# Gated-DeltaNet heads: z's sigmoid behind q's, k finished ahead of v's convolution, filler cells in other places

## The chip, the cores and the metric

The kernel runs on one core of a Trainium2 chip. The metric is the device time of one execution in microseconds (us); a kernel's time is the median of several runs. Engines are named as in the profile: TensorE (PE, and PEld for its weight loads), VectorE (DVE), ScalarE (ACT), GpSimd (POOL) and SyncE (SP).

## What is computed

Two layers of a backbone over 640 tokens (128 of context, 512 latent) of width 2048. In each layer one input projection feeds three groups of heads: four gated-DeltaNet heads (GDN), eight latent-attention heads and four mLSTM heads; an output projection joins them. The change is in the GDN heads, but for one wait. A GDN head takes q, k, v and z (128 features by 640 tokens each) out of the projection:

```python
qkv = jax.nn.silu(_centred_dwconv(jnp.concatenate([qa, ka, va], axis=-1), p['gdn_conv']).astype(f32))
q, k, v = jnp.split(qkv, [H_A * DK_A, 2 * H_A * DK_A], axis=-1)
q = _l2norm(_heads(q, H_A))
k = _l2norm(_heads(k, H_A))
...
a = jnp.where(strict, jnp.einsum('bhncd,bhnsd->bhncs', kb, k) * decay, 0.0)
t = lax.linalg.triangular_solve(a + eye, jnp.broadcast_to(eye, a.shape),
                                left_side=True, lower=True, unit_diagonal=True)
...
out = _unheads(o) * jax.nn.silu(za.astype(f32))
```

The convolution has five taps along the tokens. The inverse of a + 1, forward and backward in time, is what a head waits for before its recurrence.

## The kernel before

Every engine's program is written out by hand, in order, and engines meet at semaphores. `B.wait(engine, label)` holds the engine's queue until the other engine has done the step with that label; `B.did` marks a step, and `B.link` marks it and lets the own queue wait for its end.

**The filler.** TensorE is kept busy with the projection of the head to come: four tiles (q, k, v, z) of sixteen *cells* each. A cell is six products of 320 columns (L587 to L589); in some cells a side product (L553, four small ones) follows, eight in a tile of layer 0 and four in one of layer 1. `ahead.cells(n)` (L571) puts the next n of the 64 cells at that place of TensorE's queue, `ahead.finish()` (L810) the rest. The tiles take two banks in turn, so tile 2 (cell 32) needs `take` 0 on ScalarE (L1206), which copies tile 0 out of its bank. GpSimd splits each half of a tile's weights in two parts before TensorE can use it (L489, L494).

**A head, in order.** ScalarE issues four DMAs (L1192, L1194: the states, and two rows broadcast to all partitions), then copies q, k and v into padded tiles (L1197, L1198) once VectorE has zeroed their edges (L1620 to L1622). VectorE convolves (L1631, L1633; five steps each), ScalarE makes a sigmoid of three steps (L1080 to L1082, called at L1201, L1208, L1218), VectorE multiplies the two (`silu`, L1640, L1641). ScalarE squares q and k (L1203, L1210), TensorE sums the squares over the features (`column_sums`, L625, L626: `q sum` into wa, `k sum` into wb), ScalarE makes `q rstd` and `k rstd` (L1100, L1101), VectorE multiplies (L1650, L1652). TensorE turns k and v (L620, into wa and wb), ScalarE copies them out (L1220, L1222; the second is `v turned taken`), and VectorE begins its chain into the inverse: decays of both directions (L1661 to L1666), then the products kk and qk (TensorE, L604 in `each_tile`) times the decays (L1674, L1676), then the first block matrices of both directions, `level00` and `level10` (L1682). The solve follows: ten rounds of small block products (L613 in `each_block`), and two levels of whole products (L604), with VectorE between (L1686 to L1713). The recurrence and `o sum` (L814) end a head. In the old order TensorE's cells stand thus: 16, `q sum`, 4, `k sum`, 4, k turned, 1, v turned, 5, kk and qk, 7, the block rounds with 10, then 2, and 1 at `finish`; the ones that the change does not touch make up the 64.

**The gates**, ahead of the heads in each layer: TensorE projects four tiles (L705 to L708), the second into a bank that held the gates' own projection, which ScalarE reads in four steps (L1153 to L1156) and works on up to `log` (L1160).

## Time and profile before

| | |
|---|---|
| median of 3 runs | 3312.5 us (3311.53 to 3313.3) |
| the profiled execution | 3306.19 us, its span 3304.4 us |
| TensorE busy | 3095.8 us, 94% |
| GpSimd busy | 2080.8 us, 63% |
| VectorE busy | 1246.6 us, 38% |
| ScalarE busy | 827.9 us, 25% |
| granted TensorE clock, mean | 0.983 |

The span runs from the first to the last instruction of one profiled execution. TensorE's busy time is nearly the span, so the rest of the reading is about its idle time: which group of instructions it stood before, and what ended the wait.

### The profile page before, as it was taken

How to read it: one execution, taken by the hardware profiler on the slowest of the kernel's cores; microseconds unless marked ns; L12 is line 12 of the kernel's file. 1: busy time of each engine (PE TensorE's matmuls, PEld its weight loads, DVE VectorE, ACT ScalarE, POOL GpSimd, SP SyncE). 2: the span in 40 equal slices, each digit the busy share in tenths (PEclk: the TensorE clock that was granted, in tenths of full speed). 3: DMA queues.
4: the chain of work that ended last, by engine and by line, in shares of the span. 5: the costliest groups of instructions: out<-in, count | busy, mean ns of one | idle time of the engine just before them, and what ended most of it. 6: DMA issues, size and time to landing. Idle time of an engine off the chain costs nothing. (4 is left out here: it accounts for less than half of the span.)

```text
span 3304.4 us, 64727 instructions
## 1 busy us (share of the span) xinstructions
PE 3095.8 (94%) x27490; PEld 2791.8 (84%) x27490; DVE 1246.6 (38%) x2462; ACT 827.9 (25%) x1698; POOL 2080.8 (63%) x2507
## 2 busy tenths in 40 slices
PE   6899999999999999999997999999999999999996
PEld 1488888789999997879986988888999999787996
DVE  1245556533222114442126456655333311345112
ACT  1413423411111222331015323333111122233000
POOL 3284533546666886537877734644788788653886
PEclk9999999999999999999998999999999999999998
DMA  8533433424444221103222322322232222111322
GB/s 325 193 98 106 144 105 104 140 75 117 128 135 131 74 72 58 45 33 112 77 100 72 118 77 80 100 76 69 77 84 83 84 74 72 58 39 33 118 77 112
DMA packets 122034, 319.93 MB, mean 97 GB/s; under 512 B 18256, under 2 KB 27600, under 8 KB 120592
## 3 DMA queue, kind: packets, MB, share of 16 engines
q1 hardware_dynamic: 91008, 263.38, 25.3%
q10 hardware_dynamic: 30736, 52.40, 4.6%
q8 instruction: 216, 3.54, 0.4%
q14 instruction: 74, 0.61, 0.1%
HBM read 302.65 MB, written 13.08 MB: 96 GB/s over the span
## 5 line engine op out<-in xcount | busy, mean ns | idle before, releaser
L489 POOL TENSOR_SCALAR w_hi<-raw 128x256 fp32r<-128x256 f32 x1232 | 1066.5, 891 | 1163.8 <-PE projection L589 684.2
L494 POOL TENSOR_TENSOR w_lo<-raw,w_hi 128x256 fp32r<-128x256 f32 x1232 | 964.3, 813 | 0.0
L587 PE MATMUL projection<-h_hi,w_hi 128*128 128x320 f32 x2304 | 762.9, 331 | 7.0 <-ACTq L1323 4.0
L589 PE MATMUL projection<-h_hi,w_lo 128*128 128x320 f32 x2304 | 714.7, 310 | 0.2 <-issue 0.2
L588 PE MATMUL projection<-h_lo,w_hi 128*128 128x320 f32 x2304 | 713.9, 310 | 0.0
L534 PE MATMUL projection<-h_hi,w_hi 128*128 128x320 f32 x1984 | 616.3, 311 | 21.2 <-POOLq L499 19.0
L535 PE MATMUL projection<-h_lo,w_hi 128*128 128x320 f32 x1984 | 613.8, 309 | 0.0
L536 PE MATMUL projection<-h_hi,w_lo 128*128 128x320 f32 x1984 | 613.6, 309 | 0.0
L587 PEld LDWEIGHTS projection<-h_hi,w_hi 128*128 128x128 f32 x2304 | 435.8, 189 | 50.6 <-issue 44.1
L588 PEld LDWEIGHTS projection<-h_lo,w_hi 128*128 128x128 f32 x2304 | 436.6, 189 | 0.3 <-issue 0.3
L589 PEld LDWEIGHTS projection<-h_hi,w_lo 128*128 128x128 f32 x2304 | 434.8, 189 | 0.0
L534 PEld LDWEIGHTS projection<-h_hi,w_hi 128*128 128x128 f32 x1984 | 374.0, 188 | 24.9 <-issue 16.6
L535 PEld LDWEIGHTS projection<-h_lo,w_hi 128*128 128x128 f32 x1984 | 374.1, 189 | 0.0
L536 PEld LDWEIGHTS projection<-h_hi,w_lo 128*128 128x128 f32 x1984 | 374.0, 188 | 0.0
L1934 DVE TENSOR_SCALAR xo<-projection,mul 128x128 f32<-128x128 f32 (+2 forms) x96 | 36.3, 434 | 373.4 <-ACT work L1450 373.4
L1096 ACT ACTIVATE xo<-projection 128x640 f32<-128x640 f32 x80 | 56.6, 707 | 303.7 <-PE projection L589 196.0
L1450 ACT ACTIVATE work<-projection 128x640 f32<-128x640 f32 x32 | 22.6, 707 | 419.6 <-PE projection L536 419.6
L553 PE MATMUL projection<-fill,cond 128*32 128x128 f32 x2048 | 109.7, 286 | 2.0 <-DMA fill<-in_w_fill 2.0
L897 PE MATMUL wb<-h_hi,w_hi 128*128 128x320 f32 (+1 forms) x296 | 100.2, 338 | 9.2 <-POOLq L499 9.2
L1898 DVE TENSOR_REDUCE row_sums<-projection 128x1 f32<-128x640 f32 (+1 forms) x80 | 57.4, 718 | 133.2 <-PE projection L955 131.8
L1417 ACT ACTIVATE work<-projection,row_sums 128x640 f32<-128x640 f32 (+1 forms) x80 | 56.9, 711 | 174.6 <-DVE row_sums L1899 174.6
L978 PE MATMUL wa<-work 128*128 128x128 f32 x672 | 90.3, 278 | 9.6 <-ACT work L1424 9.6
(399 smaller groups left out, 4338.4 us busy)
## 6 DMA issues: line engine op xcount, KB each, us to landing
raw<-in_w_stream SPq DMA_DIRECT2D x308, 512.0 KB, 3.4
fill<-in_w_fill SPq DMA_DIRECT2D x256, 256.0 KB, 2.7
work<-in_w_ada SPq DMA_DIRECT2D x64, 512.0 KB, 5.1
work<-rows ACTq DMA_DIRECT2D x32, 320.0 KB, 4.1
xo<-rows ACTq DMA_DIRECT2D x32, 320.0 KB, 5.1
xo<-in_x ACTq DMA_DIRECT2D x1, 5120.0 KB, 16.7
work<-in_x ACTq DMA_DIRECT2D x16, 320.0 KB, 5.1
x_kept<-xo ACTq DMA_DIRECT2D x4, 1280.0 KB, 4.5
```

The lines of the kernel that those rows point to most:

```text
L489: nc.gpsimd.tensor_scalar(w_hi[:, s, cs, :], raw[:, s, cs, :], 1.0, None, ALU.mult).then_inc(split_part, 1)
L494: nc.gpsimd.tensor_tensor(w_lo[:, s, cs, :], raw[:, s, cs, :], w_hi[:, s, cs, :].bitcast(F32), ALU.subtract).then_inc(split_part, 1)
L534: mm(o, w_hi[:, half, c, :], h_hi[:, tile, hs], start=(k == 0), stop=False)
L535: mm(o, w_hi[:, half, c, :], h_lo[:, tile, hs], start=False, stop=False)
L536: last = mm(o, w_lo[:, half, c, :], h_hi[:, tile, hs], start=False, stop=(k == KT - 1))
L553: last = mm(bank[g * COND_W:(g + 1) * COND_W, a, HALF:HALF + P], cond[:, quad * ROW_GROUPS + g, :], fill[:, s, g, :], start=False, stop=(q ...
L587: mm(o, w_hi[:, half, c, :], h_hi[:, k, hs], start=(k == 0), stop=False)
L588: mm(o, w_hi[:, half, c, :], h_lo[:, k, hs], start=False, stop=False)
L589: last = mm(o, w_lo[:, half, c, :], h_hi[:, k, hs], start=False, stop=(k == KT - 1))
L897: mm(out, hi, xh, start=first, stop=False)
L978: last = mm(wa[:, 768:768 + P], values4[:, k0 + j, vs], T(probs_t[i % 2], j), start=(j == 0), stop=(j == nk - 1))
L1898: B.link(V.reduce_max(mxs[:, 0, t:t + 1], MLA_SCORES[i % 2][:, 0:nk], AX))
```

## The change

In the gates the second tile's projection waits for `beta exp` (L1156) where it waited for `log`. In a GDN head the four DMA issues stand behind the padding copies; z's sigmoid stands behind q's; k's square follows q's, `k rstd` comes ahead of v's sigmoid and `q rstd` behind it; `take` 0 goes behind `q rstd`. VectorE makes k's `silu` ahead of v's convolution, and norms k before v's `silu`. TensorE turns k into wb and v into wa, and v's turn waits for `q rstd` too, which reads wa. The cells stand as 16, `q sum`, 1, `k sum`, 4, k turned, 2, v turned, 2, kk and qk, 9, the block rounds with 10, then 4, and 2 at `finish`.

```diff
                     if j:
-                        B.wait("act", "log" if j == 1 else f"ahead taken{j - 2}")
+                        B.wait("act", "beta exp" if j == 1 else f"ahead taken{j - 2}")
...
                     B.did(column_sums(wa, wt(9)), "q sum")
-                    ahead.cells(4)
+                    ahead.cells(1)
                     B.wait("act", "k squared")
                     B.did(column_sums(wb, wt(11)), "k sum")
                     ahead.cells(4)
                     B.wait("dve", "k normed")
-                    B.did(transposed(wa, wt(1)), "k turned")
-                    ahead.cells(1)
+                    B.did(transposed(wb, wt(1)), "k turned")
+                    ahead.cells(2)
                     B.wait("dve", "v silu")
-                    B.did(transposed(wb, wt(4)), "v turned")
-                    ahead.cells(5)
+                    B.wait("act", "q rstd")
+                    B.did(transposed(wa, wt(4)), "v turned")
+                    ahead.cells(2)
                     B.wait("act", "v turned taken")
                     B.did(each_tile(wa, wt(1), wt(1)), "kk")
+                    B.wait("dve", "q normed")
                     B.did(each_tile(wb, wt(1), wt(0)), "qk")
-                    ahead.cells(5)
-                    ahead.cells(2)
+                    ahead.cells(9)
...
                         ahead.cells(1)
-                    ahead.cells(2)
+                    ahead.cells(4)
...
-                    for d in range(2):
-                        act.dma_start(gdn_state(d), io["state_gdn"][l, d, h, :, :]).then_inc(state_in[d], 16)
-                    for tile, kind in ((row_g[0], 0), (row_beta[0], 1)):
-                        act.dma_start(tile, rows[kind, bass.ds(h, 1), :].partition_broadcast(P)).then_inc(rows_in[0], 16)
                     B.wait("dve", "zeros")
                     for i in range(3):
                         B.did(A(pads[i][:, 2:2 + CTX], xt(4 + i)[:, 0:CTX], ACT.Copy))
                         B.did(A(pads[i][:, 6 + CTX:6 + TOK], xt(4 + i)[:, CTX:TOK], ACT.Copy), f"{'qkv'[i]} padded")
+                    for d in range(2):
+                        act.dma_start(gdn_state(d), io["state_gdn"][l, d, h, :, :]).then_inc(state_in[d], 16)
+                    for tile, kind in ((row_g[0], 0), (row_beta[0], 1)):
+                        act.dma_start(tile, rows[kind, bass.ds(h, 1), :].partition_broadcast(P)).then_inc(rows_in[0], 16)
                     for i in range(2):
                         B.wait("dve", f"{'qk'[i]} conv")
                         sigmoid(B, pads[i][:, 0:CONVW], convs[i], f"{'qk'[i]} sigmoid")
+                        if i == 0:
+                            sigmoid(B, xt(9), xt(7), "z sigmoid")
                     B.wait("dve", "q silu")
                     B.did(A(wt(9), wt(0), ACT.Square), "q squared")
-
+                    B.wait("dve", "k silu")
+                    B.did(A(wt(11), wt(1), ACT.Square), "k squared")
+                    for tile, kind in ((row_g[1], 0), (row_beta[1], 1)):
+                        act.dma_start(tile, rows[kind, bass.ds(h + 4, 1), :].partition_broadcast(P)).then_inc(rows_in[1], 16)
+                    B.wait("pe", "k sum")
+                    rsqrt(B, wt(12), wb[:, 0:TOK], wt(12), 1.0, "k rstd")
+                    B.wait("dve", "v conv")
+                    sigmoid(B, pads[2][:, 0:CONVW], convs[2], "v sigmoid")
+                    B.wait("pe", "q sum")
+                    rsqrt(B, wt(10), wa[:, 0:TOK], wt(10), 1.0, "q rstd", DK_SCALE)
                     B.wait("act", "v padded")
                     take(B, n0_, 0, xt(4))
-                    B.wait("dve", "v conv")
-                    sigmoid(B, pads[2][:, 0:CONVW], convs[2], "v sigmoid")
-                    B.wait("dve", "k silu")
-                    B.did(A(wt(11), wt(1), ACT.Square), "k squared")
-                    B.wait("pe", "q sum")
-                    rsqrt(B, wt(10), wa[:, 0:TOK], wt(10), 1.0, "q rstd", DK_SCALE)
-                    B.wait("pe", "k sum")
-                    rsqrt(B, wt(12), wb[:, 0:TOK], wt(12), 1.0, "k rstd")
-
-                    for tile, kind in ((row_g[1], 0), (row_beta[1], 1)):
-                        act.dma_start(tile, rows[kind, bass.ds(h + 4, 1), :].partition_broadcast(P)).then_inc(rows_in[1], 16)
-                    sigmoid(B, xt(9), xt(7), "z sigmoid")
                     B.wait("pe", "k turned")
-                    B.did(A(wt(2), wa[:, 0:TOK], ACT.Copy))
+                    B.did(A(wt(2), wb[:, 0:TOK], ACT.Copy))
                     B.wait("pe", "v turned")
-                    B.did(A(wt(3), wb[:, 0:TOK], ACT.Copy), "v turned taken")
+                    B.did(A(wt(3), wa[:, 0:TOK], ACT.Copy), "v turned taken")
...
                     silu(0, wt(0))
+                    silu(1, wt(1))
                     conv(2)
-                    silu(1, wt(1))
+                    B.wait("act", "k rstd")
+                    B.did(tt(wt(1), wt(1), wt(12), ALU.mult), "k normed")
                     silu(2, wt(4))
                     B.wait("act", "q rstd")
                     B.did(tt(wt(0), wt(0), wt(10), ALU.mult), "q normed")
-                    B.wait("act", "k rstd")
-                    B.link(tt(wt(1), wt(1), wt(12), ALU.mult), "k normed")
```

ScalarE at the start of the first head, before. `state` and `rows` are the DMAs' tiles, `work<-xo` the padding copies (two to a tensor), the last row the first step of q's sigmoid.

```order
L1192 DMA state<-in_state_gdn 128x128 [waits gates_act_steps,rows_out,gates_dve_steps,gates_pe_steps]
L1192 DMA state<-in_state_gdn 128x128
L1194 DMA work<-rows 128x640 x2
L1197 ACTIVATE work<-xo 128x128 [waits gdn_dve_steps]
L1198 ACTIVATE work<-xo 128x512
L1197 ACTIVATE work<-xo 128x128
L1198 ACTIVATE work<-xo 128x512
L1197 ACTIVATE work<-xo 128x128
L1198 ACTIVATE work<-xo 128x512
L1080 ACTIVATE work<-work 128x644 [waits gdn_dve_steps]
```

The same place after; its `xo<-xo` row is the first step of z's sigmoid.

```order
L1194 ACTIVATE work<-xo 128x128 [waits gates_act_steps,rows_out,gates_dve_steps,gates_pe_steps,gdn_dve_steps]
L1195 ACTIVATE work<-xo 128x512
L1194 ACTIVATE work<-xo 128x128
L1195 ACTIVATE work<-xo 128x512
L1194 ACTIVATE work<-xo 128x128
L1195 ACTIVATE work<-xo 128x512
L1197 DMA state<-in_state_gdn 128x128 x2
L1199 DMA work<-rows 128x640 x2
L1081 ACTIVATE work<-work 128x644 [waits gdn_dve_steps]
L1082 ACTIVATE work<-work 128x644 [waits gdn_act_steps]
L1083 ACTIVATE work<-work 128x644 [waits gdn_act_steps]
L1081 ACTIVATE xo<-xo 128x640
```

The copies moved ahead of the four issues, and z's steps stand where k's stood.

VectorE, from q's `silu` to z's product, as one piece of the difference: L1631 and L1633 are v's convolution, the `work<-xo,work` rows k's `silu`, L1649 k's norm in the new order (L1650 and L1652 were q's and k's).

```order
 L1640 TENSOR_TENSOR work<-work 128x128 [waits gdn_act_steps,gdn_dve_steps]
 L1641 TENSOR_TENSOR work<-work 128x512
+L1640 TENSOR_TENSOR work<-xo,work 128x128 [waits gdn_act_steps,gdn_dve_steps]
+L1641 TENSOR_TENSOR work<-xo,work 128x512
 L1631 TENSOR_SCALAR work<-work,head_conv 128x644 [waits gdn_dve_steps]
 L1633 SCALAR_TENSOR_TENSOR work<-work,head_conv 128x644 [waits gdn_dve_steps] x4
-L1640 TENSOR_TENSOR work<-xo,work 128x128 [waits gdn_act_steps,gdn_dve_steps]
-L1641 TENSOR_TENSOR work<-xo,work 128x512
-L1640 TENSOR_TENSOR work<-work 128x128 [waits gdn_act_steps,gdn_dve_steps]
+L1649 TENSOR_TENSOR work<-work 128x640 [waits gdn_act_steps,gdn_dve_steps]
+L1640 TENSOR_TENSOR work<-work 128x128 [waits gdn_act_steps]
 L1641 TENSOR_TENSOR work<-work 128x512
```

k's `silu` moved ahead of v's convolution, and k's norm between that convolution and v's `silu`.

TensorE after, from `q sum` (L625, wa) to `k sum` (L625, wb) in the first head.

```order
L625 MATMUL wa<-work,constants 128x512 [waits gdn_act_steps]
L626 MATMUL wa<-work,constants 128x128
L587 MATMUL projection<-h_hi,w_hi 128x320 [waits split_done]
L588 MATMUL projection<-h_lo,w_hi 128x320
L589 MATMUL projection<-h_hi,w_lo 128x320
L587 MATMUL projection<-h_hi,w_hi 128x320
L588 MATMUL projection<-h_lo,w_hi 128x320
L589 MATMUL projection<-h_hi,w_lo 128x320
L553 MATMUL projection<-fill,cond 32x128 [waits fill_full0]
L553 MATMUL projection<-fill,cond 32x128 x3
L625 MATMUL wb<-work,constants 128x512 [waits gdn_act_steps]
L626 MATMUL wb<-work,constants 128x128
```

One cell with its side product stands between the two sums; before there were four cells.

## Rows read from the trace of the kernel before

**Rows 1.** Page, part 1: engine, busy us (share of the span) and instructions.
```profile
PE 3095.8 (94%) x27490; PEld 2791.8 (84%) x27490; DVE 1246.6 (38%) x2462; ACT 827.9 (25%) x1698; POOL 2080.8 (63%) x2507
```

**Rows 2.** TensorE's waits: engine line, waited for, us in total, times, longest.
```profile
PE wb L613 <- issue: 23.2, 21, 2.1
...
PE wa L625 <- ACT work L1266: 15.2, 8, 2.1
...
PE wa L625 <- ACT work L1203: 9.5, 4, 3.5
...
PE wa L604 <- DVE work L1710: 3.2, 4, 1.2
...
PE wb L625 <- ACT work L1210: 1.4, 3, 0.8
```

**Rows 3.** Timeline, waiting q sums: start, us, instruction, [idle before, releaser].
```profile
494.92 0.70 PE L625 MATMUL wa<-work,constants 128*128 128x512 f32 x1 [0.80 <-ACT work L1203]
1986.07 0.70 PE L625 MATMUL wa<-work,constants 128*128 128x512 f32 x1 [1.75 <-ACT work L1203]
2103.93 0.70 PE L625 MATMUL wa<-work,constants 128*128 128x512 f32 x1 [3.46 <-ACT work L1203]
2223.92 1.00 PE L625 MATMUL wa<-work,constants 128*128 128x512 f32 x1 [3.48 <-ACT work L1203]
```

**Rows 4.** Timeline, end of layer 1's third head: ScalarE's last filler copy, TensorE's o sum.
```profile
2201.09 0.71 ACT L1096 ACTIVATE xo<-projection 128x640 f32<-128x640 f32 x1
...
2202.57 1.10 PE L625 MATMUL wa<-work,constants 128*128 128x512 f32 x2 [1.83 <-ACT work L1266]
```

**Rows 5.** Timeline, gates of layer 0: ScalarE's log, TensorE's second projection.
```profile
165.33 1.27 ACT L1160 ACTIVATE work<-work 8x1280 f32<-8x1280 f32 x1
...
179.19 0.60 PE L534 MATMUL projection<-h_hi,w_hi 128*128 128x320 f32 x1 [6.26 <-POOLq L499]
```

**Rows 6.** Timeline, ScalarE, last head of layer 1.
```profile
2208.35 0.94 ACTq L1192 DMA_DIRECT2D state<-in_state_gdn  x2
...
2210.31 0.31 ACT L1197 ACTIVATE work<-xo 128x128 f32<-128x128 f32 x1 [4.82 <-issue]
...
2220.96 0.74 ACT L1080 ACTIVATE work<-xo 128x644 f32<-128x644 f32 x1 [3.08 <-DVE xo L1633]
...
2232.15 0.80 ACT L1100 ACTIVATE work<-wb,small_constants 128x640 f32<-128x640 f32 x1 [1.05 <-PE wb L626]
...
2238.15 0.70 ACT L1222 ACTIVATE work<-wb 128x640 f32<-128x640 f32 x1 [0.67 <-PE wb L620]
```

**Rows 7.** Timeline, VectorE, last head of layer 1.
```profile
2208.68 0.17 DVE L1625 TENSOR_SCALAR head_conv<-parameters 128x5 f32<-128x5 f32 x1
...
2216.19 4.74 DVE L1633 SCALAR_TENSOR_TENSOR xo<-work,head_conv,xo 128x644 f32<-128x644 f32 x4
...
2221.58 0.68 DVE L1641 TENSOR_TENSOR work<-work 128x512 f32<-128x512 f32 x1
...
2222.90 3.70 DVE L1633 SCALAR_TENSOR_TENSOR work<-work,head_conv 128x644 f32<-128x644 f32 x4
...
2227.27 1.23 DVE L1641 TENSOR_TENSOR work<-xo,work 128x512 f32<-128x512 f32 x1
...
2251.62 1.36 DVE L1682 TENSOR_TENSOR xo<-xo,constants 128x640 f32<-128x640 f32 x1
```

**Rows 8.** Timeline, TensorE, last head of layer 1: start of the solve.
```profile
2252.76 0.33 PE L613 MATMUL wa<-constants,work 128*32 128x32 f32 x16
```

**Rows 9.** Timeline, layer 0's second head: VectorE's second block matrix, TensorE's solve.
```profile
399.61 1.01 DVE L1682 TENSOR_TENSOR xo<-xo,constants 128x640 f32<-128x640 f32 x1
...
402.59 0.41 PE L613 MATMUL wa<-constants,work 128*32 128x32 f32 x26
```

**Rows 10.** Windows behind two q sums: stretch, us, busy by engine, PEclk, DMA.
```profile
1986.06:1989.76 3.70, 3.69 (x22) 3.22 (x22) 3.56 (x5) 1.28 (x4) 3.70 (x4) 1.00 0.33 126
2223.92:2227.62 3.70, 3.70 (x11) 2.68 (x12) 3.60 (x5) 1.81 (x5) 3.70 (x5) 0.54 0.05 20
```

More of the change, by code:

```diff
@@ L1189, in _ @@
                     n0_ = int(l * STREAM_HALVES + h * 8 + (STREAM["gates"] + 8))
+                    B.wait("dve", "zeros")
+                    for i in range(3):
+                        B.did(A(pads[i][:, 2:2 + CTX], xt(4 + i)[:, 0:CTX], ACT.Copy))
+                        B.did(A(pads[i][:, 6 + CTX:6 + TOK], xt(4 + i)[:, CTX:TOK], ACT.Copy), f"{'qkv'[i]} padded")
                     for d in range(2):
@@ L1194, in _ @@
                         act.dma_start(tile, rows[kind, bass.ds(h, 1), :].partition_broadcast(P)).then_inc(rows_in[0], 16)
-                    B.wait("dve", "zeros")
-                    for i in range(3):
-                        B.did(A(pads[i][:, 2:2 + CTX], xt(4 + i)[:, 0:CTX], ACT.Copy))
-                        B.did(A(pads[i][:, 6 + CTX:6 + TOK], xt(4 + i)[:, CTX:TOK], ACT.Copy), f"{'qkv'[i]} padded")
                     for i in range(2):
```

## The prediction

> **What bounds the kernel now.** I read the page's first part, then TensorE's waits, then the timeline of one GDN head on three engines, then the granted clock. TensorE works 3095.8 us of a 3304.4 us span [rows 1], so the time is its work, which the change leaves alone, plus its waits. By cause [rows 2], the GDN heads (eight: four in each of two layers) hold five kinds. 23.2 us at L613 have no releaser and lie in the middle of products; no edit aims at them. 15.2 us stand before the `o sum` at a head's end (8 times), 9.5 before the `q sum` (4 times, up to 3.5), 3.2 before the inverse's products at L604 (4 times), 1.4 before the `k sum`. The sum below is made against the profiled execution, 3306.19 us (span 3304.4); the median of the three runs, 3312.5, lies 6.3 above it, and I take the change in us off the median.
>
> **The gates: nothing.** The second projection now waits for `beta exp`, three ScalarE steps ahead of `log`. `log` ended at 165.33 + 1.27 = 166.60, while TensorE was free for that projection at 179.19 - 6.26 = 172.93 and then waited for GpSimd's split [rows 5]. The old wait was over 6 us early; a lower mark in the same queue can't be later.
>
> **The head's end: nothing, though a cell moves there.** One more filler cell now stands before `o sum`. But ScalarE's queue has the copy of the last filler tile (L1096 at 2201.09) ahead of the square, so the square starts a fixed time after the last cell; TensorE waited 1.83 us there [rows 4], 1.9 on average over eight. A cell later in the queue delays copy, square and sum alike. The 15.2 us stay.
>
> **The head's start, worked on the last head of layer 1.** Four moves, in the order of the chain.
>
> ScalarE's four DMA issues go behind the three padding copies. They ran from 2208.35 to 2210.31, when the first copy started [rows 6]. The copies also need VectorE's zeros, which were set as L1625 began, 2208.68 [rows 7]. They can start at about 2208.8, so copies, q's convolution and all behind it come 1.5 us earlier. The issues (1.95 us) fit in ScalarE's wait for the convolution; the rows and states that they bring are read over 20 us later.
>
> z's sigmoid (three steps of 0.74, with links 2.3 us) [rows 6] now runs between q's and k's. q's ends near 2216.4, z's near 2218.7; k's convolution, whose last four steps took 4.74, ended at 2220.93 [rows 7] and will end at 2219.4. Hidden by 0.7; with the faster 3.70 of v's convolution on VectorE the cover is gone and it costs 0.3.
>
> So q's square ends 1.5 us earlier, and `q sum` starts at 2222.4. The four waits 0.80, 1.75, 3.46, 3.48 [rows 3] become 0, 0.25, 1.96, 1.98: 5.3 us less at this place.
>
> Then k is finished first. k's sigmoid ends at 2219.4 + 2.3 = 2221.7. `silu` of k follows at once (it took 2226.60 to 2228.50), to 2223.6, its square by 2224.3. TensorE has `q sum` (1.1, the length of a sum [rows 4]) and one cell, and is at `k sum` at 2224.5: no wait, and the 1.4 us of old `k sum` waits go. VectorE convolves v from 2223.6 for 4.3, to 2227.9; `k rstd` (two steps of 0.80) is ready at 2227.5, so k is normed by 2228.8, before TensorE has done its four cells. v's sigmoid ends at 2230.2, `q rstd` at 2231.9, and the filler copy `take 0`, which now stands behind them, at 2232.9. It frees the bank for the third tile, wanted some 10 us later. `v turned` has a new wait for v's `silu` (2231.7) and `q rstd` (2231.9). TensorE is there at 2222.4 + two sums (2.2) + seven cells + one turn (0.5). A cell is 1.05 us here: sixteen between 2202.57 + 1.10 = 2203.67 and 2223.92 - 3.48 = 2220.44 [rows 3, 4]. That is 2232.4, so the new wait costs nothing by 0.5. Behind `take 0` come the copies of k and of v, 0.7 each [rows 6]: `v turned taken` at 2234.3. It was 2238.85, so VectorE's chain into the inverse starts 4.5 us earlier.
>
> From there to the second block matrix VectorE needed 2252.98 - 2238.85 = 14.1 us [rows 6, 7]. That gives 2248.5, and TensorE's second block product 2248.5 where it was about 2253.1 [rows 8]: 4.6 us earlier. But three cells (3.15 us) have moved behind this point and must still be done: net 1.45. TensorE's own work would let it in sooner. From `q sum` to the solve it took 2252.76 - 2223.92 = 28.8, of which half clock lost up to 1.7 (0.46 x 3.70) [rows 3, 8, 10]; I take 1.6; less three cells that is 24.1, so it stands at the solve at 2246.5. **A new wait of about 1.5 us, split over the two first block products, takes the place of the old one.**
>
> **The other heads.** In layer 1's second and third head the same chain binds at the end, so what counts is the 1.45, not the old wait. I take 1.2 for each of the three (links between engines were left out of the chain): 3.6 us. In layer 1's first head TensorE had no wait; it arrives three cells earlier and VectorE, by the same working, only some 2.5, so I charge -0.6 (bounds -1.5 and +0.3). In layer 0 a tile carries twice the side products, TensorE is the later one at the solve by 402.59 - 400.62 = 2 us [rows 9], and moving three cells (about 3.6) against a chain 3 us earlier leaves a slack of over 1: only waits count, 0.80 of `q sum` and 1.4 - 0.8 of `k sum` (the 0.8 was in layer 1), of which I take 1.2.
>
> **Behind the solve** two of the three cells stand between the block products and the whole ones, 2.1 us of cover for VectorE's expansion. The waits at L604 were 1.2 at most [rows 2], so all 3.2 us go.
>
> **Sum:** 3.6 - 0.6 + 1.2 + 3.2 = 7.4 us; the span 3297, the median **3305**. Its own range is 4.5 to 10.5 off.
>
> **Rivals.** (1) *The wait only moves.* VectorE's chain into the inverse grows. The same `silu` step took 0.68 and, elsewhere in the head, 1.23 [rows 7]. With k's `silu`, v's convolution and its `silu` in other places relative to GpSimd's split, two such steps of 0.55 more put the second block matrix 1.1 later. Then layer 1 keeps nothing at the solve and its first head loses 1.5, while layer 0's slack covers: 1.2 + 3.2 - 1.5 = 2.9, 3309.6. For it: the chain is bare in layer 1. Against: the durations that I used are already the slow ones. The Trainium skill (SBUF — State Buffer, "Who interferes with whom") says that a VectorE instruction with two SBUF inputs and a GpSimd instruction that reads SBUF exclude each other for a whole instruction; the trace's pair agrees in direction. By that rule the loss would be up to a whole split piece at a time, by estimate about 1.6 us a head, and the time about 3311.
>
> (2) *The clock eats it.* After the 3.48 us wait the clock granted over the next 3.70 us was 0.54 (1.2 GHz for most of it); after the 1.75 us wait it stayed at 1.00 [rows 10]. The two waits of 1.96 and 1.98 and the four new ones at the solve could each cost up to 1.6: 9.6 us less gain, 3314.6. Against: the `o sum` waits are as long, eight times over. The Trainium skill (TensorE: Matmul & The Clock Gate, Part 1) says the array's clock falls to half after idling and comes back after sustained work, and that the moment is run-variable; the two stretches agree [rows 10], and by it any of the six may fall, which is this rival.
>
> (3) *Slower: ScalarE becomes the chain in every head.* If k's square is late, `k sum`, `k rstd`, v's sigmoid, `q rstd`, `take 0` and both copies all move with it, for they stand in one queue. Losing 7.4 + 6.6 us over eight heads, with 1 us of slack in the four of layer 0, asks for 8x - 4 = 14, x = 2.25 us a head: 3319 and more. k's sigmoid behind z's can be 0.3 late, k's `silu` no later than it was taken. The rows don't give 2.25.
>
> (4) *More than forecast.* The 23 us at L613 may shrink if TensorE pauses ahead of the solve, or the two half-clock stretches go without the chain binding: 12 to 15 us, 3299.
>
> **How the numbers follow.** Forecast 0.58, rival 1 0.24, rival 2 0.06, rival 3 0.05, rival 4 0.07. 0.2% is 6.6 us, about what a measurement of this kernel can tell from no change. Of the forecast's 0.58 some 0.45 lie beyond it (7.4 is close to the line), so faster 0.52, same 0.13 + 0.24 + 0.06 = 0.43, slower 0.05. The range takes in the forecast's own, rival 1 and half of rival 4: 3299.5 to 3310.5; rivals 2 and 3 and the rest of 4 are out.
>
> **What would show it.** Right: the q sum's waits fall to about 2, 2 and 0.3 in layer 1; the `k sum` row and the L1710 row vanish from TensorE's waits; a row appears at L613 with VectorE L1682 as releaser, 4 to 6 us in all, in layer 1 alone; 15 us stay before `o sum`; the gates' stretch doesn't move. Wrong: waits at L620 for `v silu` or `q rstd`, or for L1682 in layer 0 (the chain is longer than worked out: rival 1 or 3); more stretches at half clock (rival 2); waits in the middle of L613 changed by over 4 us.

## The result, and the profile after

| kernel | median, us | lowest to highest | runs |
|---|---|---|---|
| before | 3311.04 | 3302.59 to 3313.30 | 7 |
| after | 3293.61 | 3291.36 to 3300.24 | 7 |

The ratio is 0.9948, with a 95% interval of 0.9939 to 0.9958: 17.4 us less, where 7.4 were forecast. (Beside the last four kernels of the table further down, two runs of before at a granted clock of 0.75 and 0.84 are left out.) The profiled execution of after has a span of 3289.6 us (before: 3304.4). The page's busy line answers to [rows 1], and TensorE's waits (line waited for, us in total, times, longest) to [rows 2]:

```profile
PE 3092.9 (94%) x27490; PEld 2788.4 (85%) x27490; DVE 1223.9 (37%) x2462; ACT 826.0 (25%) x1698; POOL 2069.7 (63%) x2507
```
```profile
PE wb L613 <- issue: 24.2, 23, 2.3
...
PE wa L625 <- ACT work L1266: 15.2, 8, 2.1
...
PE wa L625 <- ACT work L1206: 3.5, 2, 1.8
...
PE wa L613 <- issue: 2.8, 5, 1.3
```

The rows of the `k sum` and of L1710 are gone. The `q sum` waits 3.5 us in place of 9.5. The row that the prediction expected at L613, with VectorE's L1682 as releaser, isn't there. VectorE ran the same 2462 instructions in 22.7 us less; nothing was taken away from it, and no term of the prediction's sum counts that.

The windows view from the first `q sum` to the last `o sum` of a layer holds the same work in both kernels. Its columns are stretch, us, busy time of PE, PEld, DVE, ACT and POOL with their instructions, PEclk, DMA share, GB/s. Before, layer 0 and layer 1:

```profile
247.38:716.69 469.31, 441.89 (x6611) 386.98 (x6609) 262.74 (x469) 163.29 (x378) 208.50 (x244) 1.00 0.36 111
1867.77:2320.23 452.46, 417.38 (x6135) 378.53 (x6133) 265.60 (x468) 158.98 (x364) 215.28 (x242) 0.98 0.26 82
```

After:

```profile
251.35:720.92 469.57, 444.30 (x6611) 389.06 (x6609) 250.77 (x469) 159.38 (x374) 205.00 (x243) 0.99 0.35 110
1869.13:2306.10 436.97, 413.43 (x6134) 376.11 (x6133) 255.71 (x469) 155.90 (x360) 210.16 (x242) 0.99 0.26 84
```

Layer 1 is 15.5 us shorter, VectorE's work in it 9.9 us shorter at the same count (468 and 469). Layer 0 is equal here, but this execution of before was 4.9 us below its median. Below, these two stretches are added up as "the heads": 921.8 us before and 906.5 after. A second profile of each (the run with only the gates changed, and after run again) gives 926.4 and 908.9. So the heads hold 12.9 to 19.9 us, which is the whole gain.

Most of it is idle time of TensorE: 62.5 us in before's two stretches and 48.8 in after's, 63.1 and 49.2 by the second profiles. Its busy time at the same instructions fell by 4.0 us in layer 1, where the granted clock went from 0.98 to 0.99, and rose by 2.4 in layer 0, where it went from 1.00 to 0.99. The idle time that went, by rows: `q sum` 9.5 to 3.5 (in the second profiles 7.9 to 5.3), `k sum` 1.4 (1.9) to none, L1710 3.2 (3.0) to none, and the waits in the middle of L613's products, which have a second row in before besides the one in [rows 2]:

```profile
PE wa L613 <- issue: 7.7, 11, 1.5
```

Both together went from 30.9 to 27.0 (31.6 to 25.9). No term of the prediction counts that.

The last head, by timeline rows (start, us, instruction, idle before and releaser). TensorE at the third head's `o sum`, the `q sum` of the second and third head, and the start of the last head's solve, which answer to [rows 4], [rows 3] and [rows 8]:

```profile
2194.53 1.73 PE L625 MATMUL wa<-work,constants 128*128 128x512 f32 x2 [1.83 <-ACT work L1266]
...
1984.23 1.12 PE L625 MATMUL wa<-work,constants 128*128 128x512 f32 x2 [1.76 <-ACT work L1206]
...
2099.32 2.08 PE L625 MATMUL wa<-work,constants 128*128 128x512 f32 x2 [1.75 <-ACT work L1206]
...
2237.66 0.53 PE L613 MATMUL wa<-constants,work 128*32 128x32 f32 x38
```

The last head's `q sum` starts at 2213.84 with no wait. It stands 19.3 us behind the `o sum` (before: 2223.92 - 2202.57 = 21.35), and the solve 23.8 us behind it (before 28.84), again with no wait.

### The profile page after: what moved, and what is told of

Its sections match the earlier page's. It is cut to its first block and busy times, and to the rows that moved or that the text cites. A ratio compares the mean times of both kernels' runs of the same rounds, so it can differ in the third digit from the quotient of the medians.

```text
span 3289.6 us, 64727 instructions
## 1 busy us (share of the span) xinstructions
PE 3092.9 (94%) x27490; PEld 2788.4 (85%) x27490; DVE 1223.9 (37%) x2462; ACT 826.0 (25%) x1698; POOL 2069.7 (63%) x2507
## 5 line engine op out<-in xcount | busy, mean ns | idle before, releaser
L489 POOL TENSOR_SCALAR w_hi<-raw 128x256 fp32r<-128x256 f32 x1232 | 1067.9, 892 | 1160.9 <-PE projection L589 673.7
L494 POOL TENSOR_TENSOR w_lo<-raw,w_hi 128x256 fp32r<-128x256 f32 x1232 | 952.0, 803 | 0.0
L589 PE MATMUL projection<-h_hi,w_lo 128*128 128x320 f32 x2304 | 715.0, 310 | 0.1
L589 PEld LDWEIGHTS projection<-h_hi,w_lo 128*128 128x128 f32 x2304 | 434.7, 189 | 0.7 <-issue 0.7
L553 PE MATMUL projection<-fill,cond 128*32 128x128 f32 x2048 | 111.0, 287 | 2.3 <-issue 1.1
```

Source lines behind the costliest of these rows:

```text
L489: nc.gpsimd.tensor_scalar(w_hi[:, s, cs, :], raw[:, s, cs, :], 1.0, None, ALU.mult).then_inc(split_part, 1)
L494: nc.gpsimd.tensor_tensor(w_lo[:, s, cs, :], raw[:, s, cs, :], w_hi[:, s, cs, :].bitcast(F32), ALU.subtract).then_inc(split_part, 1)
L553: last = mm(bank[g * COND_W:(g + 1) * COND_W, a, HALF:HALF + P], cond[:, quad * ROW_GROUPS + g, :], fill[:, s, g, :], start=False, stop=(q ...
L589: last = mm(o, w_lo[:, half, c, :], h_hi[:, k, hs], start=False, stop=(k == KT - 1))
```

## Why the sum was too small: the chain into the solve

Counted from the `q sum`, v's copy (L1222) ends 11.4 us later in the last head (2225.22), against 14.9 before [rows 3, 6]; the prediction had 11.9. From there to the end of the second block matrix (L1682) the prediction took 14.1 us from before [rows 6, 7]. In after it is 12.4 (2225.22 to 2236.60 + 1.02). VectorE's steps of that chain, before:

```profile
2240.64 1.25 DVE L1666 TENSOR_TENSOR work<-work,constants 128x640 f32<-128x640 f32 x1
2241.93 0.59 DVE L1661 TENSOR_SCALAR column_temps<-token_columns 128x5 f32<-128x5 f32 x1
...
2242.62 0.59 DVE L1663 TENSOR_TENSOR column_temps<-xo,column_temps 128x5 f32<-128x5 f32 x1
2243.24 1.31 DVE L1665 TENSOR_TENSOR work<-xo,column_temps 128x640 f32<-128x640 f32 x1
2244.59 0.82 DVE L1666 TENSOR_TENSOR work<-work,constants 128x640 f32<-128x640 f32 x1
```

and GpSimd's two passes over a filler tile's weights at that time (L489 has one input, L494 two):

```profile
2236.23 3.95 POOL L489 TENSOR_SCALAR w_hi<-raw 128x256 fp32r<-128x256 f32 x4 [6.32 <-PE projection L589]
2240.15 3.72 POOL L494 TENSOR_TENSOR w_lo<-raw,w_hi 128x256 fp32r<-128x256 f32 x4
...
2251.43 3.53 POOL L494 TENSOR_TENSOR w_lo<-raw,w_hi 128x256 fp32r<-128x256 f32 x4
```

After, the same engines:

```profile
2226.76 0.90 DVE L1666 TENSOR_TENSOR work<-work,constants 128x640 f32<-128x640 f32 x1
2227.70 0.24 DVE L1661 TENSOR_SCALAR column_temps<-token_columns 128x5 f32<-128x5 f32 x1
...
2228.05 0.16 DVE L1663 TENSOR_TENSOR column_temps<-xo,column_temps 128x5 f32<-128x5 f32 x1
2228.24 0.82 DVE L1665 TENSOR_TENSOR work<-xo,column_temps 128x640 f32<-128x640 f32 x1
...
2230.04 0.58 DVE L1670 TENSOR_TENSOR column_temps<-column_temps 128x5 f32<-128x5 f32 x1
...
2231.39 0.82 DVE L1674 TENSOR_TENSOR work<-wa,work 128x640 f32<-128x640 f32 x1
...
2236.60 1.02 DVE L1682 TENSOR_TENSOR xo<-xo,constants 128x640 f32<-128x640 f32 x1
```
```profile
2225.45 4.33 POOL L489 TENSOR_SCALAR w_hi<-raw 128x256 fp32r<-128x256 f32 x4 [3.38 <-PE projection L589]
2229.75 3.60 POOL L494 TENSOR_TENSOR w_lo<-raw,w_hi 128x256 fp32r<-128x256 f32 x4
```

Before, the pass L494 begins 1.3 us behind v's copy, and four steps that begin inside it take 0.35 to 0.49 longer each than the same steps of after (1.25 for 0.90, 0.59 for 0.24, 0.59 for 0.16, 1.31 for 0.82). The last one, L1682, meets the next L494 (2251.43) and takes 1.36 for 1.02 [rows 7]. That is 2.0 us. After, the pass begins 4.5 us behind v's copy. One step there is longer (L1670, 0.58 against 0.17 before). The next, L1672, came straight behind it and took 0.81 in both kernels, and L1674 and L1676 read one operand from PSUM (`wa`, `wb`) and take 0.82 as elsewhere.

GpSimd splits a filler tile when TensorE is through with an earlier one (its idle time ends on L589), so the cells set the time of L494. The prediction moved the cells and kept the chain's length.

## The experiments

All were timed in rounds beside the kernel before on the same chip. The ratio is taken over these rounds, so it can differ a little from the quotient of the two medians. "Heads" is the sum of the two stretches above, from one profile.

| kernel | us | before, us | ratio (95%) | heads, us | VectorE in them |
|---|---|---|---|---|---|
| after, again | 3291.47 | 3312.56 | 0.9939 (0.9926 to 0.9953) | 908.9 | 510.0 |
| before, one-input pass | 3344.06 | 3312.56 | 1.0093 (1.0078 to 1.0108) | 916.5 | 491.5 |
| after, one-input pass | 3330.09 | 3312.56 | 1.0060 (1.0046 to 1.0074) | 900.4 | 487.0 |
| before, DMA issues moved | 3299.96 | 3312.56 | 0.9966 (0.9954 to 0.9979) | 917.5 | 523.0 |
| after but for the DMA issues | 3296.89 | 3308.55 | 0.9967 (0.9954 to 0.9979) | 915.5 | 507.9 |
| after but for the cells | 3298.24 | 3308.55 | 0.9965 (0.9952 to 0.9977) | 915.1 | 520.1 |
| before, k's order and gates | 3314.39 | 3308.55 | 1.0017 (1.0008 to 1.0026) | 926.0 | 516.8 |
| after, o's square first | 3272.51 | 3308.55 | 0.9891 (0.9877 to 0.9904) | 886.6 | 509.2 |
| after but for z | 3309.23 | 3310.31 | 0.9994 (0.9985 to 1.0003) | 924.0 | 517.1 |
| before, cells moved | 3335.11 | 3310.31 | 1.0079 (1.0061 to 1.0096) | 949.7 | 513.8 |
| after but for k's order and gates | 3330.29 | 3310.31 | 1.0059 (1.0045 to 1.0072) | 944.3 | 511.8 |
| before, gates | 3311.12 | 3310.31 | 1.0004 (0.9992 to 1.0016) | 926.4 | 527.2 |

**After, run again**, as the measure for the rest of its chip.

> The changed kernel once more. Ratio 0.9948 to before, within 0.001. Theory A (VectorE's chain met GpSimd's second split pass less often than in the old order): in layer 1 VectorE's chain from the copy of v to the second block matrix takes 12.4 to 13 us again, and TensorE has no wait for L1682. Theory B (fewer half-clock stretches): the heads of layer 1 hold at most 10 us of half clock again, against 17 in the kernel before. Theory C (the waits inside L613 fell by chance): their sum in layer 1's heads, 12.3 us against 15.7, moves by 3 us or more from this run to the last.

It is 21.1 us below before. The heads' stretch repeats (908.9), and so does the chain: 12.4 to 12.6 us in layer 1's heads, with no wait for L1682. Layer 1's stretch is 440.11, 12.4 us below before, with three waits of 1.76 at the `q sum` in place of two. The waits in the middle of L613, which theory C calls chance, repeat: 12.0 us in layer 1 in the first profile of after (9.9 + 2.1), 12.1 here (11.5 + 0.6), against 15.5 before. As for theory B, the granted clock over layer 1 is 0.99 again, against 0.98.

**GpSimd's second pass with one input**, in the kernel before and in after. The low part of the weights is then a scaled copy and not the remainder, and VectorE meets a pass that reads one tensor:

```diff
-nc.gpsimd.tensor_tensor(w_lo[:, s, cs, :], raw[:, s, cs, :],
-                        w_hi[:, s, cs, :].bitcast(F32), ALU.subtract).then_inc(split_part, 1)
+nc.gpsimd.tensor_scalar(w_lo[:, s, cs, :], raw[:, s, cs, :], 2.0 ** -13, None, ALU.mult).then_inc(split_part, 1)
```

> The kernel before, with GpSimd's second split pass reading one SBUF tensor instead of two (the low part of the weights is a scaled copy, not the remainder, so the products' low parts are wrong and nothing else differs). Theory A: VectorE no longer waits out split pieces: k's convolution in the last head of layer 1 falls from 4.74 to about 3.7 (four steps), the chain from the copy of v to the second block matrix from 14.1 to about 12.4, the q sums' waits by about 1 us each, and the kernel by 3 to 8 us (ratio 0.9976 to 0.999). Theories B and C: these durations stay, ratio 1.000.

> The changed kernel, with the same one-input second pass (low part of the weights a scaled copy, not the remainder). Theory A: VectorE's chain is at 12.4 us already and gains at most 0.5; the q sums' waits of 1.75 fall by about 1, so 1 to 3 us below the changed kernel. If the collisions also slow GpSimd's pieces so that TensorE waits for them elsewhere (12.4 and 18.5 us of waits for the split), those shrink and both one-input kernels gain 5 us or more beyond that.

As whole times the two don't show what VectorE gains: both kernels became slower, because the pass got longer (outside the heads the kernel before takes 43 us more). The second pass by line (count, busy us, mean ns of one, idle before), in the kernel before:

```profile
L494 POOL TENSOR_TENSOR w_lo<-raw,w_hi 128x256 fp32r<-128x256 f32 x1232 | 964.3, 813 | 0.0
```

The same line with one input, and the longest row of TensorE's waits, which is now for the split and was 19.0 us in before (from here on line numbers are one lower in kernels that have a line less):

```profile
L494 POOL TENSOR_SCALAR w_lo<-raw 128x256 fp32r<-128x256 f32 x1232 | 1076.8, 874 | 97.5
```
```profile
PE projection L533 <- POOLq L498: 30.3, 49, 5.9
```

Read by stage they show what made the chain long. In the last head the steps that were long are short (again in the kernel before with this pass):

```profile
2259.93 0.90 DVE L1665 TENSOR_TENSOR work<-work,constants 128x640 f32<-128x640 f32 x1
...
2261.42 0.83 DVE L1664 TENSOR_TENSOR work<-xo,column_temps 128x640 f32<-128x640 f32 x1
```

The chain is 12.1 to 12.4 us in layer 1's heads, where before had 13.4 to 14.1, with k, v and the cells in the old order, and VectorE's time in the heads falls by 36.8 us (by 19.5 in after). So it is the two-input pass that lengthens the chain. After's own chain goes from 12.4 to 12.2, and its `q sum` row is gone, as expected; the waits for the split, which were to shrink, grew in both kernels.

How much of the change's gain hangs on this the pair doesn't settle. The two stretches with the one-input pass, before and then after:

```profile
249.04:725.32 476.28, 447.87 (x6610) 392.64 (x6609) 244.82 (x467) 162.70 (x378) 220.07 (x243) 0.98 0.35 110
1898.52:2338.70 440.18, 412.71 (x6134) 375.08 (x6133) 246.68 (x467) 158.53 (x364) 220.32 (x242) 1.00 0.26 84
...
252.03:717.94 465.91, 441.07 (x6611) 386.54 (x6609) 242.86 (x467) 159.49 (x374) 217.40 (x243) 1.00 0.35 111
1888.28:2322.77 434.49, 413.86 (x6135) 377.38 (x6133) 244.14 (x467) 155.87 (x360) 218.68 (x242) 0.99 0.26 84
```

In layer 1 the change is worth 440.18 - 434.49 = 5.7 us here, near the prediction's 5.8 for that layer (3.6 - 0.6 and 2.8 of the 3.2 at L604), and 15.5 or 12.4 with the two-input pass. But in layer 1 the clock fell from 1.00 to 0.99 here and rose from 0.98 to 0.99 there, and in layer 0 the change is worth 10.4 here. Both layers together give 16.1 us, inside the 12.9 to 19.9 of the two-input pass; whole times on this chip give 3344.06 - 3330.09 = 14.0 against 21.1. The `q sum`, `k sum` and L604 rows fall by 5.7 us here (from 4.8 + 0.9 to none), and by 10.6 or 7.5 with the two-input pass. So an estimate from these differences is that VectorE meeting the second pass less is worth 2 to 7 us: a part of what the sum left out, and not all of it. The waits in the middle of L613 fall here as well, from 33.1 to 26.6.

**The DMA issues alone, and all but them.** They go behind the copies in the kernel before; they go back ahead of them in after:

```diff
+for d in range(2):
+    act.dma_start(gdn_state(d), io["state_gdn"][l, d, h, :, :]).then_inc(state_in[d], 16)
+for tile, kind in ((row_g[0], 0), (row_beta[0], 1)):
+    act.dma_start(tile, rows[kind, bass.ds(h, 1), :].partition_broadcast(P)).then_inc(rows_in[0], 16)
 B.wait("dve", "zeros")
...
-for d in range(2):
-    act.dma_start(gdn_state(d), io["state_gdn"][l, d, h, :, :]).then_inc(state_in[d], 16)
-for tile, kind in ((row_g[0], 0), (row_beta[0], 1)):
-    act.dma_start(tile, rows[kind, bass.ds(h, 1), :].partition_broadcast(P)).then_inc(rows_in[0], 16)
```

(The diff is that of after; the kernel before has it the other way round.)

> The kernel before, with the four DMA issues alone moved behind the padding copies. The working of the prediction: each q's square 1.5 us earlier, q sum waits 9.5 -> 4.2 us, and, since all later steps stand in the old order, the whole chain 1.5 earlier in layer 1's three later heads: 4.5 to 5.5 us, ratio 0.9985. Theory B adds the half clock behind the two long waits, 3 us: ratio 0.9975. If a DMA issue costs the padding copies nothing (they overlap), ratio 1.000.

> The changed kernel with one part undone: ScalarE's four DMA issues at a head's start stand ahead of the three padding copies again, as before the change. The DMA move done alone took about 12 us off the kernel before. If the parts add up (theory 1: what the issues delay is paid in TensorE's waits for the q sum, in both kernels), the time is 9 to 13 us above the changed kernel's, about 3303, and the four q sum waits of before (9.5 us in all, up to 3.5) are back, the first of z's and k's gains staying. If the new order of k, z and the cells covers the same waits by itself (theory 2), the q sum still waits but the time stays within 4 us of the changed kernel's, 3291 to 3297.

Alone they give 12.6 us by medians, more than was expected: the `q sum` row falls by 7.7 us where 5.3 were forecast, and L1710's from 3.2 to 2.0, while the `k sum` row rises from 1.4 to 3.2. By the heads it is 4.2 to 8.9, but the two profiles of before used there (3306.19 and 3309.45) are 6.4 and 3.1 us faster than before's median on this chip; with that added it is 10.6 to 12.0. Without them after keeps 11.7 of its 17.4 to 21.1, so there they are worth 5.8 to 9.4: between the two theories of the second run. TensorE's waits for the `q sum` are 1.8 us in the first kernel and, without the move, back at

```profile
PE wa L625 <- ACT work L1206: 8.6, 3, 3.4
```

Behind the copies the issues cost nothing, since ScalarE's queue sends them out while the copies run (after, start of the last head):

```profile
2200.99 0.31 ACT L1194 ACTIVATE work<-xo 128x128 f32<-128x128 f32 x1 [2.70 <-DVE work L1622]
2201.01 0.35 ACTq L1197 DMA_DIRECT2D state<-in_state_gdn  x1
2201.20 0.62 ACT L1195 ACTIVATE work<-xo 128x512 f32<-128x512 f32 x1
2201.39 0.45 ACTq L1197 DMA_DIRECT2D state<-in_state_gdn  x1
```

**The cells: all but them, and they alone.**

```diff
-ahead.cells(1)
+ahead.cells(4)
...
-ahead.cells(2)
+ahead.cells(1)
...
-ahead.cells(2)
+ahead.cells(5)
...
-ahead.cells(9)
+ahead.cells(7)
...
-ahead.cells(4)
+ahead.cells(2)
```

This is all but them; the kernel before with them alone has the same lines the other way.

> The changed kernel with the filler cells put back where they were (4, 4, 1, 5, 7 ahead of the solve, 2 behind it, in place of 1, 4, 2, 2, 9 and 4). Prediction's working: TensorE comes to the solve three cells (3.2 us) later, VectorE's second block matrix is there by then, so no wait at the solve, but the waits at L604 for L1710 (3.2 us) are back because two cells less stand there: 2 to 5 us above the changed kernel, 3295. If the cells only move work about (their sum is the same and nothing in layer 1's heads of the changed kernel waits at the solve): within 2 us of it, 3291 to 3295.

> The kernel before with only the filler cells of the change (1, 4, 2, 2, 9 ahead of the solve and 4 behind it). TensorE comes to the solve three cells earlier, 24.1 us after the q sum in layer 1 and 26.8 in layer 0, where VectorE's second block matrix was there only after 26.9 to 29.1 us. Theory 1 (the parts need each other): waits of 2 to 4 us at the solve in all eight heads take what the three cells gave back, the cells' work comes behind instead, so no gain or a loss: 0 to 10 us above the kernel before. Theory 2 (the cells alone bring the gain, since they move GpSimd's pieces away from VectorE's chain): 4 to 8 us below it.

Without them after loses 7.1 to 10.8 us, more than either theory had. The waits at L604 return, as the first working had it:

```profile
PE wa L604 <- DVE work L1710: 3.0, 4, 1.0
```

but the rest is the chain: in the last head L494 begins 0.5 us behind v's copy, the steps are long again (L1665 1.33, L1666 1.25, L1682 1.36), and the chain is 13.9 us. In the kernel before with the new cells alone it is 12.4, although k and v have the old order. So it is the cells that move L494. Alone they cost 24.8 us all the same, and not at the solve, as theory 1 had it, but sooner: with one cell in place of four behind the `q sum`, TensorE stands at the `k sum` before k is squared (here TensorE's wait in that kernel, and in the one without k's order):

```profile
PE wb L625 <- ACT work L1209: 19.6, 8, 3.7
```
```profile
PE wb L625 <- ACT work L1211: 21.4, 8, 4.0
```

In the heads of the kernel with the cells alone TensorE's idle time is 16.9 us above before's, and its busy time 11.1 at the same count, with a granted clock of 0.98 and 0.97 in the two layers (before 1.00 and 0.98).

**k's order alone, and all but it.** The first is after with z, the cells and the DMA issues put back; the second is the kernel before with those three.

> Only the order of k, q and v (k's silu and normalising ahead of v's, the two turned banks exchanged) and the gates' wait of the changed kernel; the DMA issues, z's sigmoid and the cells are as before the change. If the parts add up and k's order is worth what the DMA move leaves of the gain (theory 1), the time is 4 to 8 us below the kernel before, about 3306, with the k sum's 1.4 us and L604's 3.2 us of waits gone and the q sum's 9.5 us still there. If k's order is only worth something once z and the cells have moved too (theory 2): within 3 us of the kernel before, 3309 to 3315.

> The kernel before with the DMA issues behind the padding copies, z's sigmoid behind q's and the new cells, but with the old order of k and v on both engines (and the old gates). Theory 1 (k's order belongs to it: v's sigmoid, q's and k's rsqrt in the old row end late): `v turned taken` ends 13 us or more after the q sum and TensorE waits 1 to 2 us at the solve in layer 1: 4 to 8 us above the changed kernel. Theory 2 (moving z off the end of ScalarE's row is enough, k's order brings nothing of its own): `v turned taken` at about 12.5, no more than 0.5 us of wait a head, within 3 us of the changed kernel's time.

Alone it loses 5.8 us, beyond both theories. z's sigmoid still stands ahead of the copies of k and v on ScalarE: v's copy ends 16.2 to 18.8 us behind the `q sum` in layer 1, the wait at L604 stays at 3.2 us, and TensorE waits at the solve in that layer's four heads:

```profile
PE wb L613 <- DVE xo L1681: 2.9, 4, 0.7
PE wa L613 <- DVE work L1681: 2.7, 4, 0.7
```

Without it the other three lose 20.0 us, with the `k sum` wait above. After, which has it, is 37.4 to 41.1 us below that kernel, beyond both theories: k's order pays for the cells that were taken from in front of the `k sum`.

**All but z**: z's sigmoid back at the end of ScalarE's row, behind `take 0`.

> The changed kernel with z's sigmoid back at the end of ScalarE's row, between the copy that frees a filler bank (take 0) and the copies of the turned k and v. Theory 1 (what counts is when v's copy, `v turned taken`, ends after the q sum): z's three steps (2.3 us) push that copy from 11.4 to 11.8 us after the q sum to about 13.9, VectorE's second block matrix from 24.0 to 26.3, and TensorE, which is at the solve 23.9 us after the q sum in layer 1, waits about 2 us there in each of its four heads; in layer 0 (26.8) hardly. 7 to 10 us above the changed kernel's time against the same kernel before, a ratio to it of about 0.997. Theory 2 (the early z only shifts k's sigmoid): nothing at the solve, within 3 us of the changed kernel.

The loss is 16 to 20 us, twice theory 1's. The solve's wait is there, smaller than thought, and one for v's copy ahead of the product of k (L604):

```profile
PE wa L604 <- ACT work L1221: 4.5, 4, 1.5
...
PE wa L613 <- DVE work L1681: 3.4, 4, 1.1
```

v's copy ends 13.0 to 13.9 us behind the `q sum` in layer 1, some two later as expected, but the chain behind it is also 13.5 to 13.8 us, since it has slid under L494 again (which begins 1.2 to 2.3 us behind v's copy). These rows and L613's other one (1.6) make 9.5 us. The heads are 15.0 to 17.4 us longer than in after's two profiles: 11.2 to 11.6 are idle time of TensorE, which is these rows and some 2 us more at L553, and 3.8 to 5.8 its busy time at the same count, with a granted clock of 0.98 in layer 1 where after had 0.99.

**The gates alone.**

> The kernel before with only the gates' second projection waiting for beta's exponential in place of the log. In the trace of before that wait ended over 6 us ahead of the next one (GpSimd's split): no change in the gates, 6.26 us at the split as before, and the time of the kernel before within 3 us. A gain of over 4 us would say that the gates hold a part of the change's gain.

Nothing (1.0004, interval 0.9992 to 1.0016). In after the second projection still waits for the split:

```profile
183.04 0.61 PE L534 MATMUL projection<-h_hi,w_hi 128*128 128x320 f32 x1 [6.26 <-POOLq L499]
```

**A further step: o's square ahead of the last filler copy**, in after:

```diff
-take(B, n0_, 3, xt(7))
 B.wait("dve", "o whole")
 B.did(A(wt(6), wt(4), ACT.Square), "o squared")
+take(B, n0_, 3, xt(7))
```

> The changed kernel, and ScalarE's square of o goes ahead of its copy of the last filler tile at a head's end. That copy holds up the square in all eight heads, and TensorE waits 15.2 us for it in all (1.9 each). If the square then ends before TensorE is at the o sum, 12 to 15 us go: about 3279. If the copy, now later, holds up something that TensorE waits for next (the bank that the next filler tile needs, or the next head's padding copies behind it on ScalarE), up to 1.0 us a head comes back: 3285 or more. If half-clock stretches set the time, it stays at 3290 to 3293.

3272.51 us, the fastest of all: 36.0 us below before and some 15 to 19 below after. The 15.2 us row is gone; the square runs at 2176.39 and the sum starts with no wait:

```profile
2178.58 1.02 PE L625 MATMUL wa<-work,constants 128*128 128x512 f32 x2
```
```profile
PE projection L587 <- ACT xo L1097: 2.5, 6, 0.5
```

The second row is what the later copy costs, 0.5 us at most each time. The gain is more than the 12 to 15 us expected: of the 20.0 to 22.4 us by which the heads are shorter than in after's two profiles, 13.6 to 14.0 are idle time of TensorE and 6.4 to 8.4 its busy time at the same count. The granted clock is 1.00 in both stretches here and 0.99 in after.

## Why the prediction was wrong, step by step

- **The gates, and the head's end: right.** 6.26 us and 15.2 us, both unchanged.
- **The DMA issues: right.** `q sum` comes 1.6 to 2.0 us earlier behind the `o sum` (forecast 1.5). That 3.5 us of the waits are left, where 4.2 were forecast, is luck: the second head kept 1.76 (forecast 0.25), the third 1.75 (1.96), the last none (1.98). The second head's 1.75 of before was short because TensorE had fallen to half clock (1.2 GHz) behind the `o sum`, and its slower cells hid the rest; in after this befell the last head, whose `o sum` took 1.73 above. Before's second `o sum`, and the granted clock (third number from the end, 0.53) behind it:

```profile
1964.84 2.05 PE L625 MATMUL wa<-work,constants 128*128 128x512 f32 x2 [1.83 <-ACT work L1266]
...
1964.70:1968.30 3.60, 3.46 (x9) 0.53 0.18 73
```

- **z hidden: right.** k's convolution ended at 2206.82 + 3.71 = 2210.53, and k's sigmoid started at 2210.59, straight behind z's: no more than 0.06 lost.
- **k first, and TensorE's own time: right.** v's copy 11.4 us behind the `q sum` (forecast 11.9), TensorE at the solve 23.8 (forecast 24.1), no wait for the `k sum`, none at L620.
- **The chain of 14.1 us: wrong, and this is the step that failed.** It was 12.4, since fewer of its steps met GpSimd's two-input pass. The block matrix, due 26.1 us behind the `q sum`, came at 23.8, as TensorE did. So the wait of "about 1.5 us, split over the two first block products", 4 to 6 us in all by the prediction's own sign, didn't come. The net 1.45 us a head, of which 1.2 was taken, was nearly 4: the three later heads took 117.75, 119.97 and 117.66 us from `o sum` to `o sum` before and 115.10, 114.83 and 111.57 after, 13.9 in all (10.9 in after's second profile) where 3.6, and 2.8 from L604, were forecast.
- **The waits in the middle of L613: a term put at nothing that wasn't.** The prediction says of them that "no edit aims at them". They went from 23.2 + 7.7 = 30.9 us to 27.0, and to 25.9 in after's second profile. The six kernels with the new cells and k's new order have 24.6 to 27.0, the six with the old cells 28.3 to 33.1, and the two with the new cells and k's old order 30.5 and 31.6. What ends these waits no run shows, so the cause stays open. By an estimate the forecast's 7.4, the 4 to 6 of the wait that didn't come and 3.9 to 5.7 here make 15 to 19 us; measured were 17.4 and 21.1.
- **The first head's loss of 0.6: wrong for the same reason.** From its `q sum` to its `o sum` it took 97.07 us, and now 95.47 (95.60 in the second profile).
- **Layer 0: right in its waits.** The 0.8 at the `q sum` and the 0.6 at the `k sum` are gone, and in its second head TensorE still comes to the solve 2.1 us behind the block matrix.
- **Rival 1 had the right mechanism with the wrong sign.** It let VectorE meet L494 more; it met it less. "The durations that I used are already the slow ones" was written as a reason against a loss, and no rival was made of a gain. Nothing in the range stood for it. The rows show that a move can gain as well as lose: steps that began inside the pass took 0.34 to 0.49 us longer, less than the whole piece (0.74) that the prediction took as the bound, and steps moved out of it got that back. The Trainium skill (SBUF — State Buffer, "Who interferes with whom") says that issue order decides who blocks. The trace has both sides waiting, VectorE beside L494 and GpSimd beside L489 (four pieces 4.33 us, and 3.30 where VectorE was idle); that the order decided which, no run here shows.
- **Rival 4 was nearest (3299), and in part by its own cause.** The waits in the middle of L613 did shrink, though TensorE doesn't wait ahead of the solve. Of the two half-clock stretches behind a `q sum` one is left in each profile of after.
- **Rival 3: not it.** No wait stands at L620.
- **Rival 2, the clock: not it.** The mean granted clock is 0.983 before and 0.984 after (1.2 GHz for a few stretches of both). The third head's `q sum` still falls to half clock behind its 1.75 us wait (2.08 us for the two matmuls, 1.12 in the second head), which costs that head 1.6 us: its solve starts 25.5 us behind the `q sum`, not 23.8. That "the `o sum` waits are as long" was no reason against it, since before's second head falls to half clock behind one.

What is open: why the waits in the middle of L613 shrink with the new order, and how much of the gain hangs on the second pass (2 to 7 us above). Single profiles of one kernel differ by 2 to 5 us here.

## What to carry to other kernels

When a change moves work that another engine reacts to (here filler cells, on which GpSimd's splits hang), the other engine's busy stretches move too: lay them beside the chain that binds, and price the chain once with them and once without. Parts of a reordering are not worth what each is worth alone: of these, the cells cost 25 us alone and save 7 to 11 with the rest, because k's order makes room for them. And a copy that stands ahead of a short step that TensorE waits for is the first thing to look for in every head: one exchanged line gave as much again as the whole change.

## What the runs showed of the hardware

- VectorE steps on SBUF that began inside GpSimd's two-input pass took 0.34 to 0.50 us longer (0.82 to 1.31 and 0.83 to 1.33 at the most), though not each of them (L1672, 0.81). Three of the four that were compared above have two inputs in SBUF; L1661 (0.59 for 0.24) has one. Beside the one-input pass it was hardly longer (0.83 to 0.90), and it was GpSimd that paid: four pieces of L489 took 4.33 us beside VectorE and 3.30 where VectorE was idle. A step with one operand in PSUM took 0.82 beside either.
- On GpSimd the one-input operation is the slower of the two at 128x256: 0.851 us a piece in the median against 0.737.
- DMA issues that stand behind queued activations go out while these run, 0.35 to 0.56 us each; ahead of them the first copy started 1.96 us behind the first issue [rows 6].
- Behind a wait of 1.83 us at an `o sum` the granted clock was 0.53 over the next 3.6 us in one head of before and 1.00 in others: waits of one length had either behind them.
